# Attention of a hybrid decoder layer: tiles of two heads alternate, turns and value products run four units after the scores

## What is computed

```python
def block(args):
    q_blk, i = args
    bias = jnp.where(dist >= 0, -slopes[:, None, None] * dist, -jnp.inf)
    scores = jnp.einsum('bhmqd,bhmkd->bhmqk', q_blk, kt).astype(jnp.float32)
    p = jax.nn.softmax(scores + bias[None, :, None], axis=-1)
    a = p[:, :, 0] - lam * p[:, :, 1]
    return jnp.einsum('bhqk,bhkv->bhqv', a.astype(vt.dtype), vt)
o = rmsnorm(o, subln_gain) * (1.0 - lambda_init)
```

## Time and profile before

| | us |
|---|---|
| median of three runs | 2255.41 |
| lowest, highest | 2250.83, 2256.68 |
| span of the profiled execution | 2253.9 |
| PE busy, share of the span | 2006.8, 89% |
| DVE busy | 1415.4, 63% |
| ACT busy | 1079.6, 48% |
| attention, from its first load to the next stage's first work | 594.8 to 1009.6, so 414.8 |

### The profile page before, as it was taken

How to read it: one execution, slowest core, us unless ns; L and a number is a source line. 1 busy time by engine, 2 the same in 40 slices (tenths; PEclk the granted TensorE clock), 3 DMA queues, 4 the chain that set the end, 5 groups by cost and what they waited for, 6 DMA issues and landing times. The chain is left out here.

```text
span 2253.9 us, 32042 instructions
## 1 busy us (share of the span) xinstructions
PE 2006.8 (89%) x10153; PEld 1672.4 (74%) x10154; DVE 1415.4 (63%) x2368; ACT 1079.6 (48%) x1591; POOL 526.0 (23%) x637
## 2 busy tenths in 40 slices
PE   6999999887798989879998599999999999999970
PEld 5887888775577868667886478888888888888850
DVE  4675677457687867856555775576668756446434
ACT  4322211325277777763222365565567655545433
POOL 2000111241000000000000244454445545334430
PEclk9999999998799999999999599999999999999985
DMA  8676986821544143005443596797879978567638
GB/s 258 214 229 200 338 280 214 279 86 47 154 109 112 35 108 75 1 18 171 146 141 126 196 370 227 271 361 249 293 260 378 347 272 314 183 235 240 209 82 308
DMA packets 170121, 458.37 MB, mean 203 GB/s; under 512 B 19872, under 2 KB 69104, under 8 KB 144432
## 3 DMA queue, kind: packets, MB, share of 16 engines
q1 hardware_dynamic: 122896, 285.30, 36.9%
q0 software_dynamic: 31008, 138.37, 20.2%
q10 hardware_dynamic: 16128, 33.56, 4.2%
HBM read 342.08 MB, written 115.10 MB: 203 GB/s over the span
## 5 line engine op out<-in xcount | busy, mean ns | idle before, releaser
L2188 DVE TENSOR_TENSOR w_down_lo<-w_down_raw,w_down_hi 128x2048 fp32r<-128x2048 f32 x64 | 144.2, 2290 | 125.3 <-ACT w_down_hi L2125 123.8
L1323 DVE CUSTOM_DVE_ANT_0 scores<-c_bank,alibi 128x512 f32<-128x512 f32 (+3 forms) x320 | 176.5, 607 | 38.9 <-PE c_bank L1434 38.6
L1460 PE MATMUL c_bank<-v_head,map_T 128*128 128x128 f32 x1088 | 149.8, 282 | 35.7 <-ACT map_T L1375 30.4
L1460 PEld LDWEIGHTS c_bank<-v_head,map_T 128*128 128x128 f32 x1088 | 133.0, 193 | 48.4 <-ACT map_T L1375 43.8
L2272 PE MATMUL m_bank<-w_down_hi,hidden_T_hi 128*128 128x512 f32 x392 | 160.4, 409 | 6.8 <-DVE w_down_lo L2188 6.8
L2188 DVE TENSOR_TENSOR w_gate_lo<-w_gate_raw,w_gate_hi 128x2048 fp32r<-128x2048 f32 x63 | 141.6, 2289 | 39.1 <-ACT w_gate_hi L2125 32.7
L2251 PE MATMUL m_bank<-w_gate_hi,rows_T_hi 128*128 128x512 f32 x392 | 156.7, 400 | 6.4 <-DVE rows_T_lo L2193 3.9
L2251 PE MATMUL m_bank<-w_up_hi,rows_T_hi 128*128 128x512 f32 x392 | 158.8, 405 | 0.0
L2252 PE MATMUL m_bank<-w_gate_lo,rows_T_hi 128*128 128x512 f32 x392 | 156.3, 399 | 0.0
L2253 PE MATMUL m_bank<-w_gate_hi,rows_T_lo 128*128 128x512 f32 x392 | 156.3, 399 | 0.0
L2188 DVE TENSOR_TENSOR w_up_lo<-w_up_raw,w_up_hi 128x2048 fp32r<-128x2048 f32 x64 | 146.2, 2289 | 15.1 <-ACT w_up_hi L2125 15.1
(11 more groups left out here) (419 smaller groups left out, 5069.5 us busy)
## 6 DMA issues: line engine op xcount, KB each, us to landing
w_gate_raw<-in_w_gate_dram SPq DMA_DIRECT2D x64, 1024.0 KB, 7.0
w_down_raw<-in_w_down_dram POOLq DMA_DIRECT2D x64, 1024.0 KB, 8.2
w_up_raw<-in_w_up_dram SPq DMA_DIRECT2D x64, 1024.0 KB, 8.2
hT_d<-hT_parts SPq DMA_DIRECT2D x32, 512.0 KB, 4.8
hT_parts<-hT_d SPq DMA_DIRECT2D x32, 512.0 KB, 9.3
k_parts<-kT_d SPq DMA_DIRECT2D x64, 256.0 KB, 8.6
u_tok<-in_x_dram SPq DMA_DIRECT2D x16, 512.0 KB, 5.7
qT_d<-qk_out ACTq DMA_DIRECT2D x32, 256.0 KB, 4.0
```

What stands on the lines that cost most here:

```text
L1323: dve.tensor_tensor_reduce(S[:, s, m, c * BANK:c * BANK + w], bank[2 * (n % 2) + m][:, 0:w], ramp[:, x0:x0 + w], SLOPES[h], -BIG, ALU.add, ...
L1460: last = pe.matmul(bank[6 + u % 2][:, 0:VD], aT[:, n % 2, b * P:(b + 1) * P], v[h % 2][:, kt], start=kt == 0, stop=kt == u % NT)
L2188: dve.tensor_tensor(wlo[w][:, halves[i]], raw[w][:, halves[i]], whi[w][:, halves[i]], ALU.subtract).then_inc(lo_done[w], 1)
```

## The change

The units get another order. Head 0's even tiles come first, rising (0, 2, ... 14). Then, for each head h, its odd tiles fall (15, 13, ... 1) in turns with the even tiles of head h + 1 rising (0, 2, ... 14), so that two neighbours always have 17 key blocks together. The odd tiles of head 3 fall alone at the end. At the first and the last such pair the two are swapped.

`turn` and `pv` come four units after the scores (three in the first eight and the last twelve units) where they came two after; `mix` comes two units after where it came one after. On ACT `exp` stays one unit after. The small sums and factors have eight slots for three. The scores of the units in flight share three places of 17 blocks for each map, a falling tile at the end of a place and its rising neighbour at the start, with hand-set places at either end. The output of a head goes straight to its place in `oT`. There is room for one more piece of keys and two more of queries, values are loaded in two parts (the first four blocks apart), and the loads are ordered by when a piece comes free. The norm comes six units after a head's last unit and `head_T` and `finish` two units after that.

```diff
@@ -1233,30 +1233,76 @@
 def attention(nc, ident, ones, shared, oT, wo, a, d):
     UN = HEADS * NT
-    SLOTS = 3
+    SLOTS = 8
     GRP = 4
-    width = lambda u: (u % NT + 1) * P
-    chunks_of = lambda u: (u % NT + 1 + GRP - 1) // GRP
+    RISE, FALL = range(0, NT, 2), range(NT - 1, 0, -2)
+    PAIR = NT + 1
+    units = [(0, i) for i in RISE]
+    for h in range(HEADS - 1):
+        for f, r in zip(FALL, RISE):
+            units += [(h, f), (h + 1, r)]
+    units += [(HEADS - 1, i) for i in FALL]
+    first, last = len(RISE), UN - len(FALL)
+    for u in (first, last - 2):
+        units[u], units[u + 1] = units[u + 1], units[u]
+    at_unit = {unit: u for u, unit in enumerate(units)}
+    head, tile = [h for h, _ in units], [i for _, i in units]
+    width = lambda u: (tile[u] + 1) * P
+    chunks_of = lambda u: (tile[u] + 1 + GRP - 1) // GRP
     pairs_before = [0]
     for u in range(UN):
         pairs_before.append(pairs_before[-1] + chunks_of(u))
-    NORM_AT = [(h + 1) * NT + 4 for h in range(HEADS - 1)]
+
+    turn_at = [u + (4 if first <= u < last - 4 else 3) for u in range(UN)]
+    turned_before = lambda n: sum(t < n for t in turn_at)
+    late_at = lambda n: [(u, c) for u in range(UN) if turn_at[u] == n for c in range(chunks_of(u))]
+
+    rise_at, fall_at = (49, 46, 41, 34, 12, 1, 21, 34), (0, 16, 30, 42, 0, 8, 16, 20)
+
+    def place_of(u):
+        if u < first:
+            return rise_at[u]
+        if u >= last:
+            return fall_at[u - last]
+        p = (u - first) // 2
+        rising = head[u] == p // len(RISE) + 1
+        return p % 3 * PAIR + (0 if rising else PAIR - tile[u] - 1)
+
+    head_end = [at_unit[h, 1] for h in range(HEADS)]
+    NORM_AT = [head_end[h] + 6 for h in range(HEADS - 1)]
+    HEAD_T_AT = [n + 2 for n in NORM_AT]
+    HELD = KSLOTS + 1
...
-        sb = Row(shared.at, 200, 206.5)
+        sb = Row(shared.at, 204, 206.5)
...
-        S = at("scores", [P, SLOTS, 2, SEQ], 52)
+        S = at("scores", [P, 2, 3 * PAIR + 1, P], 52)
+        Sf = S[:].rearrange("p m t k -> p m (t k)")
+        of = lambda u, m, c0, c1: Sf[:, m, place_of(u) * P + c0:place_of(u) * P + c1]
...
+                early, late = slice(0, GRP), slice(GRP, NT)
+                load_v(0, early)
+                for c in range(1, GRP):
+                    load_qk(0, c)
+                    if c == 1:
+                        load_v(0, late)
+                load_qk(1, 0)
                 sp.dma_start(wo[:], a["w_out"][0].rearrange("(k p) n -> p k n", p=P)[:, :, 0:BANK]).then_inc(wo_in, 16)
-                for h in range(1, HEADS):
-                    for c in range(4):
-                        sp.wait_ge(qk_done, 2 * pairs_before[NT * (h - 1) + GRP * (c + 1)])
-                        load_q(h, c)
-                        if c == 0:
-                            load_k(h, 0)
-                        if c == 1:
-                            if h >= 2:
-                                sp.wait_ge(pv_chunk, pairs_before[NT * (h - 1)])
-                            load_v(h)
-                    for c in range(1, 4):
-                        load_k(h, c)
+                load_v(1, late)
+                load_v(1, early)
+                sp.wait_ge(qk_done, 2 * pairs_before[at_unit[0, GRP] + 1])
+                load_qk(1, 1)
+                for h in range(HEADS - 1):
+                    for n, c in enumerate(reversed(range(GRP))):
+                        m = HELD + GRP * h + n
+                        if m < GRP * HEADS:
+                            sp.wait_ge(qk_done, 2 * pairs_before[at_unit[h, GRP * c + 1] + 1])
+                            load_qk(m // GRP, m % GRP)
+                    if h + 2 < HEADS:
+                        sp.wait_ge(pv_chunk, pairs_before[at_unit[h, GRP + 1] + 1])
+                        load_v(h + 2, late)
+                        sp.wait_ge(pv_chunk, pairs_before[head_end[h] + 1])
+                        load_v(h + 2, early)
...
-                    if u >= SLOTS:
-                        dve.wait_ge(mapT, pairs_before[u - SLOTS + 1])
+                    h, i, s = head[u], tile[u], u % SLOTS
+                    if turned_before(u):
...
-                for n in range(UN + 1):
+                    r = oss[:, h].rearrange("p (t o) -> p t o", o=1).to_broadcast([P, NT, VD])
+                    dve.tensor_tensor(o[h], o[h], r, ALU.mult).then_inc(fin_dve, 1)
+
+                for n in range(UN + 2):
                     if n < UN:
                         score(n)
-                    if n >= 1:
-                        mix(n - 1)
+                    if n >= 2:
+                        mix(n - 2)
...
-                for n in range(1, UN + 2):
-                    late = chunks_of(n - 2) if n >= 2 else 0
+                for n in range(1, turn_at[-1] + 1):
+                    late = late_at(n)
                     if n <= UN:
                         exp(n - 1, 0)
-                    for c in range(min(late, 2)):
-                        evacuate(n - 2, c)
-                    if n <= UN:
+                    for j, (u, c) in enumerate(late):
+                        evacuate(u, c)
+                        if j == min(len(late), 2) - 1 and n <= UN:
+                            exp(n - 1, 1)
+                        if c == chunks_of(u) - 1:
+                            rows_out(u)
+                    if not late and n <= UN:
                         exp(n - 1, 1)
-                    for c in range(2, late):
-                        evacuate(n - 2, c)
-                    if n >= 2:
-                        rows_out(n - 2)
                     if n in NORM_AT:
                         root(NORM_AT.index(n))
-                    if n - 1 in NORM_AT:
-                        finish(NORM_AT.index(n - 1))
+                    if n in HEAD_T_AT:
+                        finish(HEAD_T_AT.index(n))
...
-                for n in range(UN + 2):
+                for n in range(turn_at[-1] + 1):
                     new = chunks_of(n) if n < UN else 0
-                    late = chunks_of(n - 2) if n >= 2 else 0
-                    for c in range(min(new, 1)):
-                        qk(n, c)
-                    for c in range(max(new - 1, late)):
-                        if c + 1 < new:
-                            qk(n, c + 1)
-                        if c < late:
-                            turn(n - 2, c)
-                            if c:
-                                pv(n - 2, c - 1)
+                    late = late_at(n)
+                    if new:
+                        qk(n, 0)
+                    for j in range(max(new - 1, len(late))):
+                        if j + 1 < new:
+                            qk(n, j + 1)
+                        if j < len(late):
+                            turn(*late[j])
+                            if j:
+                                pv(*late[j - 1])
                     if late:
-                        pv(n - 2, late - 1)
-                    if n - 1 in NORM_AT:
-                        head_T(NORM_AT.index(n - 1))
+                        pv(*late[-1])
+                    if n in HEAD_T_AT:
+                        head_T(HEAD_T_AT.index(n))
```

81 lines of the change are left out of this document (41 added, 40 removed).

## The result

The change made the kernel slower: 2268.64 us (median of 4 runs, 2262.33 to 2272.69) against 2253.45 (4 runs beside them), ratio 1.0067, 95% interval 1.0041 to 1.0093. The forecast was 2260, "within 0.3%"; the range of 2243 to 2273 held it, and the measured time is that of rival B, 2268. The execution profiled has a span of 2260.7 us and is the fastest of the four.

The account below looks back on a forecast made before the run. No engine is full, so the coupling between PE, DVE and ACT decides. Start 96.0, two cycles 198.4 and end 125.1 sum to 419.5 against 414.8, +4.7 on 2255.4, giving 2260.1 us; range 2243 to 2273.

Parts of the forecast that it names:

- rival B: Slower, 2268: third key piece landing after about 618 or slow start clock, adding 8 to 10 us; chance 0.36.
- Part 1: Later mix, turn: DVE's 50.3 us waits go, ACT's chain is late, PE's map wait grows from 30.4 to above 45.
- the walk: The prediction's step by step sum over attention, carrying each engine's queue in its written order: 419.5 us.
- Part 2: Alternating wide and small tiles: 77.6 us issued, 91.8 elapsed; some 11 idle us waiting for the first evacuation.
- Part 4: Start: third key piece lands at about 616, the steady order's first tile 7 starts at 690.8; 96.0 us.
- I take 3.8: Start: us gained for tile 4's keys with 0.75 MB less ahead, so tile 4 starts at 606.5.
- Parts 3 and 5: Norm adds 7.4 us, making a cycle 99.2 us against 99.0; two steady cycles take 198.4 us.
- Part 6: End, from the third tile 7 through the unpaired falling tiles to the last norm: 125.1 us in all.
- Part 7: Shared score places: DVE's wait for a turned unit costs nothing, being covered; at most 0.44 if uncovered.
- signs of being wrong: PE idle under 8 us in a cycle (Rival A), or clock low after 622, or a cycle above 101 (rival B).
- B's two causes: Third key piece landing late in the start, 8 to 10 us; half a us more per ACT wait step, 10 us.
- Rival A: Interleaving works, PE is the bound: cycle 82.6, some 50 us gained, 2206; chance of gain over 0.3%: 0.19.

Follow-up runs that it names:

- e1: Changed kernel's new unit order with the old distances (mix one unit after the scores, turn two): 2292.19 us, ratio 1.0177.
- e2: Kernel before's unit order and loads with later work (mix two units after the scores, turn and value products three): 2244.97 us, ratio 0.9943.
- e13: The program of e5 measured again, as its edited condition dropped nothing: 2260.68 us, ratio 1.0043.
- e3: Changed kernel with ACT's first two evacuations ahead of the first exp behind a wider tile, others before the second, output rows last: 2251.98 us, ratio 1.0.
- e4: Changed kernel with the later twelve tiles of head 0's values loaded behind the third key piece: 2262.41 us, ratio 1.0038.
- e5: Changed kernel with extra PE transposes filling waits, 12 behind a much wider tile and 26 at the norm: 2264.06 us, ratio 1.0044.
- e8: Changed kernel with the edits of e3 and e4 and the norm's root made on DVE: 2241.49 us, ratio 0.9939.
- e11: e8 with the norm's multiply moved to GpSimd, head_T where it stood: 2239.92 us, ratio 0.9935.
- e10: e2 with later values behind the third key piece, root on DVE, norm's multiply on GpSimd and head_T two steps later: 2238.49 us, ratio 0.9921.

## Why the prediction was right and where it was wrong

- *Part 1, right.* DVE's wait for the exps went and PE's for the first evacuation came up. Its size was put too high: above 45 us, from 30.4, where it is 38.2, of which 12.1 in each cycle (the walk had some 11). e1 and e2 show what the distances do: 3.4 us in the old order, 28.8 in the new, where e1's clock is lower too (0.92 in its cycles).
- *Part 2, right, step by step.* The 14 steps of a cycle beside the norm's two, where the clock is up, are all within 0.3 us of the walk (7.67 for 7.8, 8.17 for 8.1, 6.41 for 6.3, 7.16 for 7.1), e13's cycle is 99.3 for 99.2, and e3 shows that ACT's order causes the wait for the map, by taking 7.3 of its 12.1 us a cycle away.
- *Part 4, mis-sized by 3.6 us.* The step that failed is the landing of the third piece, 4 MB "which at these rates land at about 616". It landed 24.7 us after the start for 21.2; by the clock of rows 1 that is 619.5, beyond rival B's "about 618". From there to the first tile 7 the walk has 74.8 us and the trace 74.9. The walk counted only the bytes ahead of the piece. In those 24.7 us the transfer engines moved 4.7 MB (171 and 220 GB/s in the two windows above, 192 in the mean), and 4.2 MB stand ahead (the prediction's 4, in units of 10^6 bytes), so some 0.5 MB of other transfers took some 3 us (an estimate from these numbers). e4, with less ahead of the piece, brings it 3.8 us earlier. "I take 3.8" for tile 4's keys was too much as well, 1.6 (15.5 to 13.9 us): less was ahead, but the loads ran at 171 GB/s to that point where the kernel before had 211. This cost nothing in the sum, as PE waits for the third piece behind it in any case.
- *Parts 3 and 5, wrong in one assumption, 4.5 us.* "Two cycles from there: 198.4 us" carried the clock at 1.00, as before had it. The norm's two steps (tiles 4 and 9) were walked at 17.6 us and took 19.3, with PE standing 4.1 us and the clock at 0.50 behind it; in e13, with the clock up, they take 17.7. In the second cycle tiles 1 and 14 cost another 1.6 us by a slow stretch. The walk contained the waits; what they did to the clock was not asked. Rival B had a slow clock, but only in the start.
- *Part 6, 2.1 us.* The step with two late units took 10.9 us for 9.6. In e5, e8 and e11 it takes 9.4 or 9.5; with the windows low at 937 in the changed kernel these 1.3 us are mostly the clock. The other 0.8 us are spread over the end.
- *Part 7, right*: no wait at the shared places is found.
- *Sum.* +4.7 forecast, 3.6 + 4.5 + 2.1 missing, +14.9 in the trace, +15.2 in the medians. So the change is slower by more than 0.3%, which was B's outcome and not the forecast's, and the prediction's own signs of being wrong came true: the clock is low after 622 and a cycle takes over 101 us. Of B's two causes one is there (the third piece) and the other is not (waits half a us longer); the clock in the cycles took that one's place. That the time fell within 1 us of B's 2268 is luck.
- *Rival A* and the rule of the Trainium skill (Perfetto Trace Analysis, Optimization Strategy): interleaving regimes can gain. No run reaches 82.6 us a cycle. But once ACT's order, the root and the multiply are out of the way the interleaved cycle is the shorter, 92.2 against 94.8 with the clock at 1.00 in both (e11 and the first cycle of e10). The rule holds inside the cycle; it says nothing of the price at start and end, where the tiles have no partner and wide ones need keys early.

What stays open: how the slow stretches depend on the program. They are shown to cost 1.4 to 3.4 us a cycle here. They lay elsewhere in e4, where one load is moved, but also between two executions of one program, so e4 does not show that the load moved them. No version was made that is free of them in start, cycles and end at once.

## What to carry to other kernels

Before reordering units for balance, walk the in-order engine that sits between the two you want to balance: here another order of ACT's work in some steps was worth 12.7 us where the reordering cost 18.3. Split such a change and measure its halves; the cheap half (work taken up a unit later) was a gain by itself. Count what else the transfer engines carry, not only the bytes ahead of a piece. Look at which steps an edit's condition really leaves out: e13's left out none. And where a walk shows the matrix engine standing for microseconds, price the slower clock behind the wait too, and a start and an end that have no partner.

## What the runs showed of the hardware

- A wait of PE of 3.4 to 4.1 us can be followed by matmuls at half clock (0.63 for 0.40 us, some five microseconds long at 776), or not, with the same wait to 0.1 us; so can one of 1.88 us, in the same step of one execution.
- GpSimd's multiply of 128 x 2048 took 3.61 us where 5.3 was estimated from a product of 510 columns. While it runs, one kind of DVE instruction stands. The timeline of e11:

```profile
764.15 3.61 POOL L1367 TENSOR_TENSOR attn_T<-attn_T,root_y 128x2048 f32<-128x2048 f32 x1 [249.94 <-DVE root_y L1413]
```

```profile
765.26 0.29 DVE L1383 CUSTOM_DVE_ANT_0 scores<-c_bank,alibi 128x128 f32<-128x128 f32 x1
765.88 0.17 DVE L1395 RECIPROCAL row_inv<-row_sum 128x2 f32<-128x2 f32 x1
766.08 1.71 DVE L1397 SCALAR_TENSOR_TENSOR map_scale<-row_sum,neg_lambda,row_inv 128x1 f32<-128x1 f32 x1
767.82 0.62 DVE L1399 SCALAR_TENSOR_TENSOR scores<-scores,map_scale 128x384 f32<-128x384 f32 x1
```

  Scores (one input from a bank) and the reciprocal (one input) run at their usual times; the first instruction with two inputs in SBUF, usually 0.22 us, ends with GpSimd's, at 767.8. In e10 the same instruction takes 1.43 us and ends with GpSimd's too. The Trainium skill (GPSIMD Engine Reference, Key points) says that GpSimd shares its SBUF interfaces with VectorE, with contention for instructions with two SBUF inputs; the row agrees, 1.5 us of the 2.3 saved.
- Tile 4's keys landed 9.2 to 9.4 us after their last request was issued in the kernel before, the changed kernel and e4 (requests issued until 6.2, 4.6 and 5.0 us after the start), with 2.6, 1.8 and 1.8 MB to be loaded up to them. The third piece landed 10.1 us after its last request in the changed kernel and 9.0 in e4. Why it takes this time isn't shown.
